# Scores of distances 2 to 16 from products of 64 keys by 32 queries on two column groups; own-key and distance-one scores from elementwise products summed by ones

## What is computed

```python
b = jnp.cumsum(gc, axis=2)
diff = b[:, :, :, None, :] - b[:, :, None, :, :]
decay = jnp.exp(jnp.where(causal, diff, -jnp.inf))
scores = jnp.einsum('bhtd,bhsd,bhtsd->bhts', qc, kc, decay)
o = o_inter + jnp.einsum('bhts,bhsv->bhtv', scores, vc)
```

## Time and profile before

| | us |
|---|---|
| median of 3 runs | 830.75 (830.71 to 831.6) |
| the profiled execution | 830.96 |
| its span | 828.4 |
| TensorE busy in it | 786.7 |
| VectorE, ScalarE, GpSimd busy | 246.6, 154.1, 120.8 |
| mixer, until the experts begin | about 367 |

### The profile page before, as it was taken

One profiled execution on the slowest core, in us unless ns is written; L12 is line 12 of the kernel. 1 busy time (PEld: TensorE's weight loads), 2 busy tenths in 40 slices (PEclk: granted clock), 3 DMA queues, 4 the chain that ended last, 5 costly groups with the idle time before them and its releaser, 6 DMA issues.

```text
span 828.4 us, 9578 instructions
## 1 busy us (share of the span) xinstructions
PE 786.7 (95%) x3929; PEld 453.0 (55%) x3929; DVE 246.6 (30%) x528; ACT 154.1 (19%) x242; POOL 120.8 (15%) x139
## 2 busy tenths in 40 slices
PE   6999999999999999999999999999989988999996
...
GB/s 302 255 102 148 232 158 204 194 188 192 191 285 408 247 302 102 115 306 416 422 398 429 426 427 426 426 425 428 426 429 425 428 427 429 427 423 421 423 419 109
DMA packets 74388, 267.99 MB, mean 324 GB/s; under 512 B 5598, under 2 KB 37450, under 8 KB 58335
## 3 DMA queue, kind: packets, MB, share of 16 engines
...
q0 software_dynamic: 528, 1.90, 0.6%
...
## 4 chain that ended last, share of the span: by engine, by line
PE 78%; DMA 13%; POOL 3%; DVE 2%; issue 2%; ACT 1%; SPq 1%; DVEq 0%; POOLq 0%
PE bank L1889 22%; PE bank L1529 21%; PE bank L1927 11%; DMA slots<-in_w_expert_gate_dram 8%; PE bank L1785 7%; PE bank L1936 6%; DMA slot<-in_w_expert_gate_dram 4%; PE bank L1732 2%; PE bank L1572 2%; DMA slots<-in_w_in_dram 1%; PE bank L1916 1%; DVE early L1396 1%; ACT wrep L953 1%; PE bank L1853 1%; PE bank L1800 1%
## 5 line engine op out<-in xcount | busy, mean ns | idle before, releaser
L1529 PE MATMUL bank<-hT,slots 128*128 128x264 f32 x896 | 207.2, 391 | 0.2 <-DMA slots<-in_w_in_dram 0.2
L1889 PE MATMUL bank<-slots,hT 128*64 128x512 f32 x680 | 185.6, 595 | 7.7 <-DMA slots<-in_w_expert_gate_dram 7.7
L1529 PEld LDWEIGHTS bank<-hT,slots 128*128 128x128 f32 x896 | 170.0, 192 | 28.9 <-issue 0.6
L1396 DVE TENSOR_TENSOR early<-early,bank 128x512 f32<-128x512 f32 x16 | 11.0, 688 | 384.6 <-PE bank L1889 384.6
L1889 PEld LDWEIGHTS bank<-slots,hT 128*64 128x64 f32 x680 | 57.1, 137 | 109.0 <-issue 96.9
L1927 PE MATMUL bank<-slots,wrep 128*64 128x512 f32 x336 | 103.6, 596 | 5.4 <-ACT wrep L953 5.4
L1889 PE MATMUL bank<-slot,hT 128*64 128x512 f32 x256 | 73.7, 594 | 2.3 <-DMA slot<-in_w_expert_gate_dram 2.3
L767 POOL COPY hT<-early 128x512 f32 x30 | 17.6, 613 | 369.6 <-PE bank L1889 286.3
L1936 PE MATMUL bank<-hT,diag 128*128 128x512 f32 x128 | 59.2, 605 | 0.2 <-ACT hT L965 0.2
L1927 PEld LDWEIGHTS bank<-slots,wrep 128*64 128x64 f32 x336 | 32.1, 137 | 49.7 <-issue 41.0
L1098 DVE SCALAR_TENSOR_TENSOR slot<-slot,rows_buf 128x256 f32<-128x256 f32 x120 | 48.1, 478 | 0.0
...
## 6 DMA issues: line engine op xcount, KB each, us to landing
...
```

What stands on the lines that cost most here:

```text
L1396: dve.tensor_tensor(act.rearrange("s (f c) -> s f c", f=FT), act.rearrange("s (f c) -> s f c", f=FT), bank[UP][:, :].rearrange("s (c f) -> ...
L1529: last = mm(out, w[:, a, t * P:(t + 1) * P], hT[:, a, :], start=(a == 0), stop=(a == KT - 1))
L1889: last = mm(out[sl, :], xe[:, a, sl], expert_view(p, kind, e, a // 4)[:, a % 4, :], start=(a == 0), stop=(a == KT - 1))
```

## The change

- Own keys: GpSimd multiplies all queries and keys of the prompt (own_key_products, 2048 elements a lane, into the place that the values by token take later). TensorE sums over the channels with 32 columns of ones, once for each of four column groups, 512 columns each. VectorE multiplies 32 by 32 blocks with the identity (8 instructions in place of 4). Since this writes blocks only, GpSimd clears score early on.
- Level 0: the same with two column groups of 64, both tiles in one bank (4 products of 256 columns in place of 2 of 512).
- Levels 1 to 4 (distances 2 to 16): 64 keys by the 32 later queries of the same half tile, on column groups at 0 and 64, both tiles in one bank: 32 products in place of 16, in one go. The masked copy works on 64 lanes (4 instructions of 256 elements in place of 2 of 512).
- Level 5 does the same products as before, both tiles in one go. Level 6 and the cross scores are unchanged.
- Three semaphores of constants become one, and two sums of GpSimd wait on another counter.
- GpSimd's order: own_key_products after decayed_qk(0); decayed_qk(2) ahead of conv_sum, decayed_qk(3) ahead of square_sum.

Core of the diff:

```diff
+        qk_all = slot6[:, 0:2 * D].rearrange("p (h t) -> p h t", h=HEADS)
...
-        score_items = [("diag", g) for g in range(4)]
-        score_items += [("lv", i, t) for i in range(len(LEVELS)) for t in range(2)]
+        score_items = ["diag"] + [("lv", i) for i in range(len(LEVELS) - 1)]
+        score_items += [("lv", len(LEVELS) - 1, t) for t in range(2)]
...
+            pool.wait_ge(misc.ready, misc.written(("x", KT - 1)))
+            pool.memset(score[:, :, :], 0.0).then_inc(score_clear, 1)
...
-                    pool.wait_ge(scores.ready, scores.written(("lv", i - 2, 1)))
+                    pool.wait_ge(scores.ready, scores.written(last_of(i - 2)))
...
+            def own_key_products():
+                pool.tensor_tensor(qk_all, q[:, :, 0:SEQ], k[:, :, 0:SEQ], ALU.mult).then_inc(qk_ready, 1)
 
             decayed_qk(0)
+            own_key_products()
             decayed_qk(1)
+            decayed_qk(2)
             conv_sum()
-            decayed_qk(2)
+            decayed_qk(3)
             square_sum()
-            decayed_qk(3)
...
-            def score_dst(g, off=None):
-
-                h0, t = 4 * (g % 2), g // 2
-                c = (0, SEQ)[t] if off is None else off
-                return score[:, h0:h0 + 4, c:c + P]
+            def lane_blocks(n):
+                return [slice(b, b + n) for b in range(0, P, n)]
+
+            def score_block(t, lanes):
+                c0 = (0, SEQ)[t]
+                return score[lanes, :, c0 + lanes.start:c0 + lanes.stop]
 
             def upper(x, i):
                 return x.rearrange("p a (n x) -> p a n x", x=2 * LEVELS[i])[:, :, :, LEVELS[i]:]
 
-            def level_take(i, tiles):
-                for t in tiles:
-                    src = take(scores, ("lv", i, t))
-                    h = LEVELS[i]
+            def level_take(i):
+                src, h = take(scores, ("lv", i)), LEVELS[i]
+                dve.wait_ge(*scores.read(("lv", i - 1) if i else "diag"))
+                for t in range(2):
                     c0 = (0, SEQ)[t]
-                    if h == P // 2:
-                        dve.tensor_copy(score[0:h, :, c0 + h:c0 + P], src[0:h, :].rearrange("p (a x) -> p a x", a=HEADS)).then_inc(S_dve, 1)
-                    elif h == QUARTER:
+                    if h == QUARTER:
+                        part = src[:, t * SEQ:(t + 1) * SEQ].rearrange("p (a x) -> p a x", a=HEADS)
                         for b in (0, 2 * h):
-                            last = dve.tensor_copy(score[b:b + h, :, c0 + b + h:c0 + b + 2 * h],
-                                                   src[b:b + h, 0:HEADS * h].rearrange("p (a x) -> p a x", a=HEADS))
-                        last.then_inc(S_dve, 1)
-                    else:
-                        kept = upper(masks[:, i, :].unsqueeze(1).broadcast_to([P, HEADS, P]), i)
-                        data = src[:, :].rearrange("p (a n x) -> p a n x", a=HEADS, x=h)
-                        dve.copy_predicated(upper(score[:, :, c0:c0 + P], i), kept, data).then_inc(S_dve, 1)
+                            last = dve.tensor_copy(score[b:b + h, :, c0 + b + h:c0 + b + 2 * h], part[b:b + h])
+                        continue
+                    part = src[:, t * SEQ:(t + 1) * SEQ].rearrange("p (a n x) -> p a n x", a=HEADS, x=h)
+                    for lanes in lane_blocks(2 * QUARTER):
+                        kept = masks[lanes, i, lanes].unsqueeze(1).broadcast_to([2 * QUARTER, HEADS, 2 * QUARTER])
+                        last = dve.copy_predicated(upper(score_block(t, lanes), i), upper(kept, i), part[lanes])
+                last.then_inc(S_dve, 1)
+
+            def top_level_take(t):
+                i, h, c0 = len(LEVELS) - 1, LEVELS[-1], (0, SEQ)[t]
+                src = take(scores, ("lv", i, t))
+                dve.tensor_copy(score[0:h, :, c0 + h:c0 + P], src[0:h, :].rearrange("p (a x) -> p a x", a=HEADS)).then_inc(S_dve, 1)
 
...
-            def diag_take(g):
-                src = take(scores, ("diag", g))
-                dve.tensor_tensor(score_dst(g), src[:, :].rearrange("p (a c) -> p a c", a=4),
-                                  ident[:, :].unsqueeze(1).broadcast_to([P, 4, P]), ALU.mult).then_inc(S_dve, 1)
+            def diag_take():
+                src = take(scores, "diag")[:, :].rearrange("p (a t x) -> p a t x", a=HEADS, t=2)
+                for t in range(2):
+                    for lanes in lane_blocks(QUARTER):
+                        own = ident[lanes, lanes].unsqueeze(1).broadcast_to([QUARTER, HEADS, QUARTER])
+                        last = dve.tensor_tensor(score_block(t, lanes), src[lanes, :, t, :], own, ALU.mult)
+                last.then_inc(S_dve, 1)
 
...
-            diag_take(0)
             o_samples(0)
             level_diff(2)
-            diag_take(1)
             o_rows(2)
             tap(4)
-            diag_take(2)
+            dve.wait_ge(c_masks, len(LEVELS))
+            dve.wait_ge(score_clear, 1)
+            diag_take()
             o_samples(2)
             level_diff(3)
-            tap(2)
-            diag_take(3)
-            dve.wait_ge(*scores.read(("diag", 3)))
+            level_take(0)
             o_rows(4)
-            tap(10)
-            dve.wait_ge(c_masks, len(LEVELS))
-            level_take(0, (0,))
+            tap(12)
             o_samples(4)
             tap(CT * TAPS)
-            level_take(0, (1,))
             o_rows(6)
-            level_take(1, (0,))
+            level_take(1)
             o_samples(6)
 
...
-            def level(i, t):
+            def level(i):
                 pe.wait_ge(kq_ready, i + 1)
-                item = ("lv", i, t)
+                item, h = ("lv", i), LEVELS[i]
                 scores.before_write(pe, item)
-                out = bank[scores.bank(item)]
-                h, m = LEVELS[i], P if LEVELS[i] < P // 2 else P // 2
-                if i == 0:
-                    last = mm(out[:, :].rearrange("p (a n) -> p a n", a=HEADS), ones[:, 0:P],
-                              kq[0][:, :, t * P:(t + 1) * P].rearrange("p a (n x) -> p a n x", x=2)[:, :, :, 1], start=True, stop=True)
-                for a in range(HEADS) if i else ():
+                out, m, n = bank[scores.bank(item)], 2 * QUARTER, QUARTER
+                for t in range(2):
+                    for a in range(HEADS) if i else ():
+                        x = kq[i % 2][:, a, t * P:(t + 1) * P]
+                        if h == QUARTER:
+                            for b in (0, 2 * h):
+                                c = t * SEQ + a * h
+                                last = mm(out[b:b + h, c:c + h], x[:, b:b + h], x[:, b + h:b + 2 * h], start=True, stop=True,
+                                          tile_position=(0, b))
+                            continue
+                        c = t * SEQ + a * n
+                        for b in (0, m):
+                            late = x[:, b:b + m].rearrange("p (n x) -> p n x", x=2 * h)[:, :, h:]
+                            last = mm(out[b:b + m, c:c + n].rearrange("p (n x) -> p n x", x=h), x[:, b:b + m], late,
+                                      start=True, stop=True, tile_position=(0, b))
+                    for b in () if i else (0, m):
+                        late = kq[0][:, :, t * P + b:t * P + b + m].rearrange("p a (n x) -> p a n x", x=2)[:, :, :, 1]
+                        last = mm(out[b:b + m, t * SEQ:(t + 1) * SEQ].rearrange("p (a n) -> p a n", a=HEADS),
+                                  ones[:, 0:m], late, start=True, stop=True, tile_position=(0, b))
+                last.then_inc(S_ready, 1)
+
+            def top_level(t):
+                i, h = len(LEVELS) - 1, LEVELS[-1]
+                pe.wait_ge(kq_ready, i + 1)
+                scores.before_write(pe, ("lv", i, t))
+                for a in range(HEADS):
                     x = kq[i % 2][:, a, t * P:(t + 1) * P]
-                    if h == QUARTER:
-                        for b in (0, 2 * h):
-                            last = mm(out[b:b + h, a * h:(a + 1) * h], x[:, b:b + h], x[:, b + h:b + 2 * h], start=True, stop=True,
-                                      tile_position=(0, b))
-                        continue
-                    last = mm(out[0:m, a * (P // 2):(a + 1) * (P // 2)].rearrange("p (n x) -> p n x", x=h), x[:, 0:m],
-                              x.rearrange("p (n x) -> p n x", x=2 * h)[:, :, h:], start=True, stop=True)
+                    last = mm(bank[scores.bank(("lv", i, t))][0:h, a * h:(a + 1) * h], x[:, 0:h], x[:, h:], start=True, stop=True)
                 last.then_inc(S_ready, 1)
 
-            def diagonal(g):
-                pe.wait_ge(q_ready, 1)
-                tile_scores(("diag", g), k, q)
+            def diagonal():
+                pe.wait_ge(qk_ready, 1)
+                scores.before_write(pe, "diag")
+                out = bank[scores.bank("diag")]
+                for b in range(0, P, QUARTER):
```

(15 more changed lines are left out.)

81 lines of the change are left out of this document (34 added, 47 removed).

## The result

| | before | after |
|---|---|---|
| median, us | 830.73 (830.01 to 831.6, 4 runs) | 841.21 (837.81 to 842.23, 4 runs) |
| the profiled execution, its span | 830.96, 828.4 | 837.81, 836.0 |
| TensorE, VectorE, GpSimd busy | 786.7, 246.6, 120.8 | 780.6, 264.4, 126.2 |

The account below looks back on a forecast made before the run. It took TensorE, nearly full in the mixer, to be held by VectorE and GpSimd blocking each other and by late value loads. TensorE's work falls 7.5 us, waits grow some 10: +3.0 on 830.75 gives 833.8 us, range 829.5 to 838.0.

Parts of the forecast that it names:

- TensorE's work: Mixer: 19.2 us of products removed and 11.7 us added, so TensorE's own work falls by 7.5 us.
- The wait at o_samples(4): TensorE, there at 135.3 us, waits 5.4 us for VectorE's copy of o_rows(4), delayed beside GpSimd's products.
- Rival 3: Levels 2 to 16: column pairs don't overlap, 0.134 us a product, total +6 us, 836.8; chance 0.12.
- var: After centring, square and sums of 2.0 to 2.9 us, var comes at 162.1 us against 158.19 before.
- updates: First sixteen state updates: GpSimd no longer pauses, so seven take 15.5 us and nine 2.5, ending at 191.7 us.
- states_add(2) end: VectorE, 11.6 us of work behind the first updates: ends at 203.3 us against 197.4 before.
- last values: Last value loads go out 5.9 us later and land at 222.2 to 224.3 us, against 218.4 before.
- The cross products: TensorE, waiting for GpSimd as before, starts them at 230.7 to 232.8 us: +1.9 to +3.9, taken as +3.0.
- rival 4: TensorE's clock may drop behind a wait of 5 us, 2.3 us on top, total 836; chance 0.06.
- Rivals 1 and 2: Total: about 822 us, VectorE and GpSimd disturbing each other less (chance 0.14); or near no change, say 831 (0.26).
- Rival 1: TensorE is not made to wait and reaches the cross products at 219.3 us; total about 822; chance 0.14.

Follow-up runs that it names:

- e3: Changed kernel without own_key_products, TensorE summing the queries themselves in its place, so own-key scores differ; median 832.1 us.
- e5: Kernel before with only own keys and level 0 as changed, levels 1 to 5 and GpSimd's order as before; median 832.3 us.
- e6: Changed kernel with GpSimd's order of before (conv_sum ahead of decayed_qk(2), square_sum ahead of decayed_qk(3)); median 835.0 us.
- e2: Changed kernel with VectorE waiting for GpSimd's square sum before level_diff(4); median 839.4 us.
- e4: Kernel before with only levels 1 to 5 as changed; median 834.5 us, and 834.6 us when profiled again.
- g4: Changed kernel with GpSimd's old order, o_rows(4) before level_diff(3), VectorE waiting for the square sum, GpSimd for states_add(0) and level_diff(4); median 828.0 us.
- g2: Kernel before with only levels 1 to 5 as changed, plus GpSimd waiting for states_add(0) ahead of sample_head(2); median 831.6 us.

## Why the prediction was right and wrong

Forecast 833.8 us (829.5 to 838.0), slower; measured 841.2, 10.5 us over before where 3.0 were forecast. The direction held, the size did not. Step by step, predicted against the profiled execution:

- TensorE's work: levels 2.15 us each, measured 2.0; own keys 0.95, measured 1.00; level 0 0.95, measured 1.05; work -7.5, busy time -6.1. Right. Rival 3, serial pairs, fell: 0.062 us a product, not 0.134. The Trainium skill's rule in "TensorE: Matmul & The Clock Gate", section "LDWEIGHTS", taken one load after the other, would have given 3.4 us a level; the row has 1.99.
- The wait at o_samples(4): 5.4, measured 5.76. Right, with its causes: e3, e5 and e6 show the product and decayed_qk(2), and that they don't add up, since the product also pushes level_diff(3) beside decayed_qk(2).
- **var: 162.1, measured 166.6. This is the step that failed.** The centring ended at 160.0, not 157.9, since all in front was 2 us later: mean came at 154.5, not 152.5. VectorE's copy gives 0.9 of that (diag_take 3.44 in place of 2.8, level_take(0) 2.93 in place of 2.6), and the clock behind the first wait about 1.3. And the two sums took 5.4 us, not 2.0 to 2.9, since VectorE's two differences in a row held the first one out. e2, where the sums run first, takes 2.7 us of it back at var. The trace of before already had the pattern: a sum of 0.75 us took 3.59 beside two differences. GpSimd, then VectorE, before:

```profile
154.55 3.59 POOL L715 TENSOR_TENSOR slot<-slot 128x264 f32<-128x264 f32 x1
```

```profile
155.19 1.20 DVE L1061 TENSOR_TENSOR slots<-early 128x1024 f32<-128x1024 f32 x1
156.32 1.21 DVE L1062 TENSOR_TENSOR slots<-early 128x1024 f32<-128x1024 f32 x1
```

- From var on the steps held, 4.5 us later: values asked for at 167.4, landed 8.9 us later (9 forecast); updates 17.6 us (18.2); states_add(2) end 207.9 (203.3); last values 17.2 us under way (16.9 to 18.9). ga was not in the sum: ScalarE's wait for the store follows states_add(2). The cross products came at 236.6, not 230.7 to 232.8. 833.8 + 4.5 = 838.3, and the profiled execution has 837.8. That a delay at var passes on whole is not certain, though: in e2 0.8 of 2.7 us did. And the updates' 17.6 us are one of two outcomes, as e4's two executions show; the forecast knew of one.
- **The clock was rival 4 at 0.06, added to nothing.** This is the second step that failed. It fell behind the first wait, which cost 1.4 us in the profiled execution (4.63 + 1.11 against 3.73 + 0.60; it is part of the 4.5 us above), and behind three waits in the other one, which took 3.2 us more. The median is 3.4 us above 837.8. The other three executions of the result have lower mean granted clocks (0.984 to 0.988 against 0.995) but no traces, so that they lost their time in the same places is not shown. I had argued from granted clocks of 1.00 in stretches where TensorE never waited more than 2 us, which say nothing of a wait of five.
- Rivals 1 and 2 fell: VectorE and GpSimd disturb each other more than computed, not less. Rival 1's outcome, TensorE made to wait little before the cross products, is near to what g4 shows once the order lets it (0.9, 1.0 and 0.4 us before them), at 828 us and not at its 822. (Its 7.7 us of saved work are 7.5 in the sum above it.)

Not shown: which of VectorE and GpSimd gets the port when both have work at hand, why g2's runs still spread over 7 us, and what decides whether the clock falls behind a wait (it didn't behind 3.52 us at var in one execution, and did behind 3.50 in the other).
